# A gate stage in another order: sums of h on VectorE, block sums by DMA, and the softplus ahead of the last sigmoids

## The reference

```python
proj = h @ w_in                        # h: 512 x 1024
gq, gk, gv, gg, glr, hq, hf, hi, hg, ma, mb = split(proj)
log_alpha = log_sigmoid(glr @ w_gk2 + b_gk2) / 16
o_a = chunk_gated_linear_attn(gq, gk, gv, log_alpha)    # GLA, 4 heads
y_a = rmsnorm(o_a, gla_norm_w) * silu(gg)
o_b = chunk_gated_linear_attn(silu(hq), key, hi, log(f))  # HGRN2, 8 heads
y_b = rmsnorm(o_b, hgrn_norm_w) * silu(hg)
merged = sigmoid(ma) * y_a + sigmoid(mb) * y_b
```

## Time and profile before

| what | value |
|---|---|
| median of 3 runs (lowest, highest) | 905.46 us (904.32, 905.64) |
| profiled execution, its own time | 906.95 us |
| its span in the trace | 905.2 us |
| mean granted clock of TensorE | 0.986 |
| TensorE busy (matmul) | 866.2 us, 96% |
| VectorE busy | 613.8 us, 68% |
| ScalarE busy | 490.3 us, 54% |
| GpSimd busy | 263.4 us, 29% |

### The profile page before, as it was taken

The page is one execution under the profiler, slowest core; times in us unless marked ns, Lnnn a source line. Parts: engine busy times, 40 slices in busy tenths (PEclk is TensorE's granted clock), DMA queues, the critical chain, the costliest instruction groups (busy, mean ns, idle before and its releaser), DMA issues.

```text
span 905.2 us, 12744 instructions
## 1 busy us (share of the span) xinstructions
PE 866.2 (96%) x4688; PEld 714.3 (79%) x4688; DVE 613.8 (68%) x775; ACT 490.3 (54%) x740; POOL 263.4 (29%) x231
## 2 busy tenths in 40 slices
PE   7988999979899899999999999999999999999997
PEld 6766788758688688788888787888888888888885
DVE  3589969637884885786574547655544444599995
ACT  5557455367655845856576544543333333366574
POOL 2164849441320312113152300111221111343300
PEclk9999999989999999999999999999999999999999
...
DMA packets 149235, 130.21 MB, mean 144 GB/s; under 512 B 4743, under 2 KB 132065, under 8 KB 148928
## 3 DMA queue, kind: packets, MB, share of 16 engines
...
...
## 4 chain that ended last, share of the span: by engine, by line
PE 81%; DVE 11%; issue 3%; ACT 3%; POOL 2%; DMA 0%; ACTq 0%; DVEq 0%; POOLq 0%
PE ps L2185 16%; PE ps L2187 16%; PE ps L2186 16%; PE ps L2615 4%; PE ps L2613 4%; PE ps L2614 4%; PE ps L2420 3%; PE ps L2422 3%; PE ps L2421 3%; PE ps L2266 2%; DVE w_lo L1612 2%; PE ps L2508 1%; PE ps L2509 1%; PE ps L2512 1%; PE ps L2332 1%
## 5 line engine op out<-in xcount | busy, mean ns | idle before, releaser
L2185 PE MATMUL ps<-h_hi,w_hi 128*128 128x512 f32 (+1 forms) x568 | 224.8, 396 | 6.2 <-DVE w_lo L1831 6.2
L2187 PE MATMUL ps<-h_hi,w_lo 128*128 128x512 f32 (+1 forms) x568 | 220.7, 389 | 0.0
L2186 PE MATMUL ps<-h_lo,w_hi 128*128 128x512 f32 (+1 forms) x568 | 220.7, 389 | 0.0
L2185 PEld LDWEIGHTS ps<-h_hi,w_hi 128*128 128x128 f32 x568 | 107.6, 189 | 29.1 <-DVE w_lo L1831 6.6
L2186 PEld LDWEIGHTS ps<-h_lo,w_hi 128*128 128x128 f32 x568 | 107.6, 189 | 22.5 <-issue 1.0
L2187 PEld LDWEIGHTS ps<-h_hi,w_lo 128*128 128x128 f32 x568 | 107.5, 189 | 21.9
L976 POOL TENSOR_TENSOR prod<-conv 128x512 f32 x21 | 43.3, 2060 | 219.8 <-DVE conv L2027 219.8
L1378 ACT ACTIVATE conv<-ps,vecs 128x512 f32<-128x512 f32 x42 | 32.6, 778 | 132.2 <-PE ps L2187 123.9
L2023 DVE SCALAR_TENSOR_TENSOR conv<-ps,vecs,conv 128x511 f32<-128x511 f32 x44 | 33.0, 749 | 104.8 <-ACT conv L1378 102.3
L1831 DVE TENSOR_TENSOR w_lo<-raw,w_hi 128x1024 fp32r<-128x1024 f32 x46 | 59.3, 1304 | 61.4 <-ACT w_hi L1018 61.4
L874 POOL TENSOR_TENSOR qs<-qs,qry 128x512 f32<-128x512 f32 x12 | 17.4, 1452 | 169.0 <-ACT qs L1166 129.5
(11 more groups left out here) (309 smaller groups left out, 1834.8 us busy)
## 6 DMA issues: line engine op xcount, KB each, us to landing
...
```

What stands on the lines that cost most here:

```text
L2185: pe.matmul(dst, a_hi, b_hi, start=start and i == 0, stop=False)
L2186: pe.matmul(dst, a_hi, b_lo, start=False, stop=False)
L2187: last = pe.matmul(dst, a_lo, b_hi, start=False, stop=stop and i == n - 1)
```

## The change

It reorders the units of the gate stage and moves work between engines; what is computed stays the same.

- The order of the block products (`G_PASSES`): pair 1's G11 now follows pair 0's G21, and pair 2's G11 stands ahead of pair 1's GA22. G21 of pair 1 moves from behind GS3 to behind pair 0's GS3.
- The four sums of h go from GpSimd to VectorE (`left_sum`), between the lows of units 2 to 6 (`SUM_STEP`). GpSimd keeps the two multiplications of each gate tile.
- The sum of two blocks for GS1 goes from VectorE to GpSimd's accumulating DMAs (`add_block`, six more blocks in all); VectorE's `g_sum` remains for GS2.
- Tables replace the rule "six units behind": `STASH_AT`, `FOLD_STEP`, `SIG_STEP`, `COMB_STEP`. Some stashes and the fold of G21 of pair 0 come one to three units later.
- SP loads the blocks in the order `G_ORDER` and the first block of pair 1 ahead of its write of xT.
- At the end of the stage `gla_z(0)` stands ahead of the last weighing, and softplus ahead of the last two sigmoids. The memset of `sT` stands ahead of the gate tiles of the last three block products, the reduction into `stack` behind the first decays, and ScalarE's exponentials of group 0 ahead of its evacuation of product (0, 1) instead of (0, 6).
- In groups 0 to 2 `gla_z(g + 1)` moves between the two calls of `times_k`, ahead of the last `silu` of its group.

```diff
-G_PASSES = ([(0, p) for p in (G11, G21, GS1, GS2, GS4, GS3)] + [(1, G11), (0, GA22)]
-            + [(1, p) for p in (GS1, GS2, GS4, GS3, G21, GA22)]
-            + [(2, p) for p in (G11, GS1, GS2, GS4, GS3, G21, GA22)])
+G_PASSES = ([(0, G11), (0, G21), (1, G11)] + [(0, p) for p in (GS1, GS2, GS4, GS3)] + [(1, G21), (0, GA22)]
+            + [(1, p) for p in (GS1, GS2, GS4, GS3)] + [(2, G11), (1, GA22)]
+            + [(2, p) for p in (GS1, GS2, GS4, GS3, G21, GA22)])
...
-G_SUMS = {GS1: (0, 1), GS2: (0, 2)}
-G_PLACES = ((0, 2, 3, 1), (1, 3, 2, 0), (2, 3, 0, 1))
+G_PLACES = ((0, 2, 3, 1), (1, 2, 0, 3), (3, 2, 0, 1))
+G_ORDER = ((0, 3, 2, 1), (0, 3, 1, 2), (0, 2, 1, 3))
...
+STASH_AT = {g_end(q, p) + RING + {(0, G11): 1, (1, G11): 3}.get((q, p), 0): (q, p) for q, p in G_PASSES if p in G_STASHED}
+FOLD_STEP = {g_end(q, p) + RING + {(0, G21): 2}.get((q, p), 0): (q, p) for q, p in G_PASSES if p in G_OUTS}
+SIG_STEP = {j + 1: at for j, at in FOLD_STEP.items()}
+COMB_STEP = {4: 0, 6: 1, 8: 2, 10: 3}
+SUM_STEP = {2: (0,), 4: (1,), 6: (2, 3)}
...
             for j in range(NG):
...
+                q, p, i = G_UNITS[j]
+                if j in SIG_STEP:
+                    g_gate(*SIG_STEP[j])
+                if p == G11:
+                    pool.wait_ge(lo_made, PIECES + j + 1)
+                    if q:
+                        pool.wait_ge(hi_made, PIECES + 2 * G_PASSES.index((q - 1, GS1)) + i + 1)
+                    add_block(q, 1, i, block_at(q, 0, i), t_added[4 + i])
+                if p == GS1 and q or p == G21 and q == 0:
+                    pool.wait_ge(*block_count(q, 1, i))
                     add_block(q, 2, i, block_at(q, 1, i), t_added[i])
-                q, p, i = G_UNITS[j]
                 if p == GS2:
                     pool.wait_ge(lo_made, PIECES + j + 1)
                     add_block(q, 3, i, block_at(q, 0, i), t_added[2 + i])
+            g_gate(PAIRS - 1, GS4)
+            pool.wait_ge(proj_done, PIECES + g_end(PAIRS - 1, GS4) + 1)
+            pool.memset(sT[:], 0.0).then_inc(mask_made, 1)
             for p in (GS3, G21, GA22):
-                g_gates(PAIRS - 1, p)
-            pool.wait_ge(proj_done, PIECES + NG)
-            pool.memset(sT[:], 0.0).then_inc(mask_made, 1)
+                g_gate(PAIRS - 1, p)
...
+            side_sigmoids(PAIRS - 1, GS4)
+            split_hi_g(0, 0)
+            split_hi_g(0, 1)
+            side_sigmoids(PAIRS - 1, GS3)
+            side_sigmoids(PAIRS - 1, G21)
+            softplus(0)
+            side_sigmoids(PAIRS - 1, GA22)
             for g in range(GROUPS):
                 group(g)
...
+            def left_sum(a):
+
+                src, op = ((3, ALU.subtract), (0, ALU.add), (1, ALU.subtract), (1, ALU.subtract))[a]
+                if a in (1, 2):
+                    dve.wait_ge(a_made, a)
+                dve.tensor_tensor(left_full(a), left_full(src), left_full(a), op).then_inc(a_made, 1)
...
+            for j in range(NG, NG + RING + 3):
+                if j in FOLD_STEP:
+                    g_out(*FOLD_STEP[j])
+                if j == NG:
+                    split_lo_g(0, 0)
+                if j == NG + 2:
+                    split_lo_g(0, 1)
+                if j == max(FOLD_STEP) - 1:
+                    gla_z(0)
             dve.wait_ge(mask_made, 5)
-            dve.wait_ge(side_sig, NT)
...
                         times_k(g, 1)
+                        gla_z(g + 1)
                         times_k(g, 2)
                         split_lo_g(*SPLIT_AT[g][n][1])
```

More of the change, by code:

```diff
@@ L253, in g_added @@
     return 32 * (q + 1)
-G_END = {g_end(q, p): (q, p) for q, p in G_PASSES}
+G_OUTS = (GS4, GS3, G21, GA22)
+STASH_AT = {g_end(q, p) + RING + {(0, G11): 1, (1, G11): 3}.get((q, p), 0): (q, p) for q, p in G_PASSES if p in G_STASHED}
+FOLD_STEP = {g_end(q, p) + RING + {(0, G21): 2}.get((q, p), 0): (q, p) for q, p in G_PASSES if p in G_OUTS}
+SIG_STEP = {j + 1: at for j, at in FOLD_STEP.items()}
+GATE_STEP = {j + 3: at for j, at in FOLD_STEP.items()}
+COMB_STEP = {4: 0, 6: 1, 8: 2, 10: 3}
+SUM_STEP = {2: (0,), 4: (1,), 6: (2, 3)}
+assert len(STASH_AT) == 3 * PAIRS and len(FOLD_STEP) == 4 * PAIRS
 ADA_STEPS = {0: (7, 7, 12, 13), 1: (1, 2, 3, 3, 4, 4, 5, 6), 2: (1, 2, 3, 3, 4, 4, 5, 6),
@@ L739, in _ @@
             sp.wait_ge(start_act, 8)
-            for k in (0, 3):
+            for k in G_ORDER[0][:2]:
                 for i in range(2):
@@ L1023, in block_hi @@
                 q, p, i = G_UNITS[j]
-                if p in G_SUMS:
-                    act.wait_ge(t_made, 4 * q + 2 * (p == GS2) + i + 1)
-                elif p in (GS3, GA22):
-                    act.wait_ge(t_added[i if p == GS3 else 2 + i], g_added(q))
+                if p == GS2:
+                    act.wait_ge(t_made, 2 * q + i + 1)
+                elif p in (GS1, GS3, GA22):
+                    act.wait_ge(t_added[{GS3: 0, GA22: 2, GS1: 4}[p] + i], g_added(q))
                 else:
@@ L1139, in _ @@
             for j in range(2, NG):
-                if j - RING in G_END and G_END[j - RING][1] in G_STASHED:
-                    stash_product(*G_END[j - RING])
-                q, p, i = G_UNITS[j]
-                if q == 0 and i == 0 and p in (GS1, GS2, GS4, GS3):
-                    comb_high((GS1, GS2, GS4, GS3).index(p))
-                block_hi(j)
-                if j - RING - 1 in G_END and G_END[j - RING - 1][1] in (GS4, GS3, G21, GA22):
-                    side_sigmoids(*G_END[j - RING - 1])
-            split_hi_g(0, 0)
-            side_sigmoids(PAIRS - 1, GS4)
-            split_hi_g(0, 1)
-            side_sigmoids(PAIRS - 1, GS3)
-            side_sigmoids(PAIRS - 1, G21)
-            side_sigmoids(PAIRS - 1, GA22)
+                if j in STASH_AT:
+                    stash_product(*STASH_AT[j])
+                if j in COMB_STEP:
+                    comb_high(COMB_STEP[j])
+                block_hi(j)
+                if j in SIG_STEP:
+                    side_sigmoids(*SIG_STEP[j])
             def exps(g, h, inv):
@@ L1843, in _ @@
             for j in range(2, NG):
-                if j - RING in G_END and G_END[j - RING][1] in (GS4, GS3, G21, GA22):
-                    if j - RING == min(g_end(0, p) for p in (GS4, GS3, G21)):
+                if j in FOLD_STEP:
+                    if j == min(FOLD_STEP):
                         dve.wait_ge(nw_in, 32)
@@ L1850, in _ @@
                         dve.wait_ge(xT_out, 16)
-                    g_out(*G_END[j - RING])
-                q, p, i = G_UNITS[j]
-                if q == 0 and i == 0 and p in (GS1, GS2, GS4, GS3):
-                    comb_low((GS1, GS2, GS4, GS3).index(p))
+                    g_out(*FOLD_STEP[j])
+                if j in COMB_STEP:
+                    comb_low(COMB_STEP[j])
                 block_lo(j)
-                if j + 2 < NG and G_UNITS[j + 2][1] in G_SUMS:
-                    g_sum(j + 2)
-            split_lo_g(0, 0)
-            g_out(PAIRS - 1, GS3)
-            split_lo_g(0, 1)
-            g_out(PAIRS - 1, G21)
-            g_out(PAIRS - 1, GA22)
+                if j == 2:
+                    dve.wait_ge(h_full_made, KT)
+                    dve.wait_ge(lr_done, 1)
+                for a in SUM_STEP.get(j, ()):
+                    left_sum(a)
+                if j + 2 < NG and G_UNITS[j + 2][1] == GS2:
+                    g_sum(j + 2)
+            for j in range(NG, NG + RING + 3):
+                if j in FOLD_STEP:
+                    g_out(*FOLD_STEP[j])
+                if j == NG:
[4 more added lines that the diff above has]
+                    gla_z(0)
             dve.wait_ge(mask_made, 5)
-            dve.wait_ge(side_sig, NT)
-            dve.tensor_reduce(stack[:], ident[:].rearrange("p (b j) -> p j b", j=32),
-                              mybir.AxisListType.X, ALU.add).then_inc(stack_made, 1)
             def group(g):
@@ L1939, in group @@
                             hgrn_y(g, t)
-                    if late:
-                        gla_z(g + 1)
-                        if g + 2 < GROUPS:
-                            next_gk2(g + 2)
+                    if late and g + 2 < GROUPS:
+                        next_gk2(g + 2)
             for g in range(GROUPS):
```

45 lines of the change are left out of this document (14 added, 31 removed).

## The result

The changed kernel took 898.1 us (median of 4 runs, 897.2 to 899.0) beside 904.9 for the kernel before (4 runs): a ratio of 0.992, 95% interval 0.991 to 0.994. It is faster by 6.8 us, where 14.4 were forecast; the time lies in the range of 884 to 900. The profiled execution took 898.95 us, its span is 897.2.

What follows compares the result with a forecast made beforehand. It took TensorE's waits, mostly for VectorE's late hand-ordered queue, and the lower clock behind them as the bound. Gate stage 5.3, its end 7.4 and gla_z 1.7 make 14.4 us: 891.1 us, range 884 to 900.

Steps and rivals of the forecast that it cites:

- the landing of unit 4's block: Gate stage, pair 1's G11: block lands at 62.4, so TensorE waits 0.9 us, bounds none and 6.
- Unit 10: Gate stage: TensorE waits 1.4 us for a stash behind the fold of G21 and two sigmoids.
- Units 7, 8, 12 and 16: Gate stage: late lows, a late stash and a late fold make TensorE wait 0.9, 0.6, 0.3 and 2.0 us.
- Unit 28: Gate stage, pair 1's GA22: its fold stands behind unit 30's accumulated block, issued at 124.5; wait 0.2 us, bounds 0 and 11.
- rival B: Gate stage: GpSimd is the late queue, unit 28 waits 4 us and the clock falls once; 896.7 us, chance 0.2.
- The end of the stage: Gate stage to group 0: earlier gla_z(0) and softplus cut the 6.2 us wait before product (0,6); gain 7.4 us.
- rival E: End of the gate stage gives less, through ScalarE delays or late weights: 4.1 us more, 895.2 us, chance 0.11.
- gla_z: Changes of group: with gla_z moved ahead, silu ends the waits and the next product starts 0.55 us earlier, three times: 1.7.
- Sums of h: Start of gate stage: on VectorE its sums take 1.21 us instead of 3.4, and the first wait (3.5 us) goes.
- Rival D: Gate stage: accumulating DMAs hold up in-order queues, unit 28 waits 11.3 us; 908 with 4 us before unit 34; chance 0.07.

Runs made afterwards that it cites:

- e1: The changed kernel, with GpSimd issuing its four accumulating DMAs for pair 0's GS3 only when the blocks of units 4 and 5 have landed: 892.0 us.
- e11: The changed kernel, with pair 0's two block sums for GS1 on VectorE again and GpSimd's four DMAs for GS3 waiting for them: 891.2 us.
- e5: The changed kernel, with the stash count for which TensorE and VectorE wait following ScalarE's order of stashes; no instruction moved: 899.5 us.
- e6: e1 with the stash count of e5, and the stash of pair 0's GS1 one unit earlier on ScalarE: 893.7 us.
- e13: e12 with the stashes of GS1 and GS2 of all three pairs one unit earlier on ScalarE: 892.6 us.
- e3: The kernel before, with only the end of the gate stage as in the changed kernel: 898.7 us.
- e8: e1 with the four sums of h back on GpSimd, behind its first four DMAs: 895.0 us.
- e9: e1 with the folds of GS3 of all three pairs one unit earlier on VectorE: 892.6 us.
- e10: e6 with pair 0's GA22 sigmoids one unit later, pair 0's GS2 stash earlier, pair 1's G11 stash two units later, and the folds of e9: 894.6 us.
- e12: e10 with pair 0's block sums for GS1 on VectorE as in e11, in place of the later DMAs: 891.7 us.
- e15: e13 with the sigmoids and GpSimd's gate tiles of GS3 back where the changed kernel has them: 885.0 us.
- e4: The kernel before, with only gla_z moved between the two calls of times_k at the three changes of group: 902.3 us.
- e14: The changed kernel with the order of stashes, folds and sigmoids of e13, its eight early accumulating DMAs left as they were: 896.7 us.

## Why the prediction failed, step by step

- **The step that failed** is the landing of unit 4's block: "Beside GpSimd's accumulating DMAs such a pair landed 4.1 and 5.4 us after issue, which gives 62.4". That pair had two such DMAs begun ahead of it (the three of before begin at 63.41, the pair at 64.6), and this one has eight, begun within 5.2 us. Its two DMAs landed 6.5 and 8.6 us after issue, and ScalarE got it at 65.4. The bounds (0 to 6 us of waiting) held the 4.3; the value taken did not, and the clock behind the wait, another 2.9 us (5.46 + 3.31 for two units in place of 2.95 each), was not in the sum. Together that is 6.3 us of the 7.8 by which the gate stage missed. With what units 10 and 28 took beyond the forecast (3.2 and 1.3), less the 3.4 of units 7, 8, 12 and 16 that did not come, it is 7.4. e1 and e11 show the cause; with four DMAs ahead the wait is the forecast's 0.9 (e1).
- **Unit 10** was forecast at 1.4 us and took 3.0 and 1.6 of clock. The chain (fold, two sigmoids, stash) was right; that TensorE waits by a count for one more stash was missed, and it is 1.9 us of it (the two pairs in ScalarE's rows above, and e5).
- **Units 7, 8, 12 and 16** were to wait 0.9, 0.6, 0.3 and 2.0. In the changed kernel unit 8 waits 0.4 and the others nothing, as TensorE was already late. Where TensorE is earlier they come back (0.5 each at 7 and 8 in e1, 1.9 at 12 and 0.9 at 16 in e6): the queues there are tight, at 12 more and at 16 less than counted.
- **Unit 28**, the new tie, was forecast at 0.2 and took 1.5. The mechanism is right; GpSimd issued at 130.2, not 124.5, and idle before it, 2.5 us, ended with VectorE's low, not with its own backlog. So rival B's cause was not seen here, though GpSimd's order did decide e13. That the time, 898.1, came out near B's 896.7 is chance.
- **The end of the stage** was right: 6.9 for 7.4 us, 6.2 in the trace of e3. The extra table load costs its 1.28 us and no more; these rows of ScalarE in the changed kernel show it 0.02 us behind Ln, and the sigmoid 0.02 us behind it:

```profile
190.52 0.72 ACT L1175 ACTIVATE lg<-lg,cols 128x512 f32<-128x512 f32 x1
191.26 1.28 ACT L1078 ACT_TABLE_LOAD   x1
192.56 1.09 ACT L1078 ACTIVATE sg<-ps 128x512 f32<-128x512 f32 x2
```

  The drain that the Trainium skill counts (ScalarE: Activation LUTs, What ACT_TABLE_LOAD costs) is not in this row either, so rival E loses its support.
- **gla_z** gave 3.4 for 1.7. Silu ends the waits as forecast (5.0 us for 7.0), which is worth 2.0. The other 1.3 is clock: behind the second change before, TensorE ran at 0.65 (the third row of before above), and in this execution at full clock. The windows of the earlier trace rows had not been read there. This part is luck of the execution: with the new order the clock behind the second change fell in 7 of 15 profiles (e6, e8, e9, e10, e12, e13 and e15) and not in the others, e4 among them. In both profiles with the old order it fell once, before at the second change and in e3 at the third; whether the move makes a fall rarer is not shown.
- **Sums of h**: instructions at 1.22 us, first wait gone, 2 to 3 us by e8; the mechanism was right.
- Rival D put a tie of this kind, a stash behind a high that waits for an accumulated block, at unit 34. One came up at unit 36 once the gate tiles had been put ahead of the block's DMAs (3.0 to 3.7 us in e10, e12, e13 and e14); with the changed kernel's order of tiles it isn't there.

By terms: forecast 5.3 + 7.4 + 1.7 = 14.4; by the trace -2.5 + 6.9 + 3.4 = 7.8, of the span's 8.0.
